# Second block: row splits shared by ScalarE and VectorE at three places, products of the identity in idle stretches of TensorE, and a reordered last layer norm of the first block

## What is computed

```python
for l in range(DEPTH):                      # block 1
    x = layer_norm(ALPHA * x + hybrid_mixer(x), ...)
    x = layer_norm(ALPHA * x + hier_moe(x), ...)
# block 2: u = norm(x) * (1 + scale) + shift, with a scale and a shift for each column
x = norm(ALPHA * x + gain * gla(u));  x = norm(ALPHA * x + gain * relu(u @ w1)**2 @ w2)
x = norm(ALPHA * x + gain * ssd(u));  x = norm(ALPHA * x + gain * relu(u @ w1)**2 @ w2)
```

## Time and profile before

| | us |
|---|---|
| three runs: median (lowest to highest) | 2241.13 (2236.27 to 2246.55) |
| the profiled execution: time / span | 2240.53 / 2238.3 |
| mean granted clock of TensorE | 0.961 of 2.4 GHz |
| TensorE (PE) busy | 2014.4 (90% of the span) |
| weight loads (PEld) busy | 1447.9 (65%) |
| VectorE (DVE) / ScalarE (ACT) / GpSimd (POOL) busy | 1229.2 / 729.5 / 167.2 |

### The profile page before, as it was taken

The page is one execution under the profiler, slowest core; times in us unless marked ns, Lnnn a source line. Parts: engine busy times, 40 slices in busy tenths (PEclk is TensorE's granted clock), DMA queues, the critical chain, the costliest instruction groups (busy, mean ns, idle before and its releaser), DMA issues.

```text
span 2238.3 us, 30881 instructions
## 1 busy us (share of the span) xinstructions
PE 2014.4 (90%) x12070; PEld 1447.9 (65%) x12070; DVE 1229.2 (55%) x2175; ACT 729.5 (33%) x1316; POOL 167.2 (7%) x155
## 2 busy tenths in 40 slices
PE   7989889879998778969998999999989988998997
PEld 4776433327785323326886788888867776777896
DVE  3474411134473212147466686666667876877676
ACT  3452201014552101124324311121165437654332
POOL 2001100001002000015422100000100000000000
PEclk9999999989998999988999999999999998999999
DMA  7589699975597899952221332232222342324552
GB/s 237 179 287 337 262 409 405 371 300 177 197 364 260 333 393 402 364 193 76 76 76 76 107 119 102 87 113 76 84 76 90 109 151 94 132 108 165 198 188 95
DMA packets 151921, 440.23 MB, mean 197 GB/s; under 512 B 10369, under 2 KB 12849, under 8 KB 143457
## 3 DMA queue, kind: packets, MB, share of 16 engines
q1 hardware_dynamic: 142704, 412.72, 49.3%
q0 software_dynamic: 8352, 22.39, 3.5%
q10 hardware_dynamic: 720, 3.15, 0.3%
HBM read 534.52 MB, written 1.21 MB: 239 GB/s over the span
## 4 chain that ended last, share of the span: by engine, by line
PE 40%; DVE 7%; ACT 4%; DVEq 2%; issue 1%; DMA 1%; ACTq 0%; POOL 0%; SPq 0%; POOLq 0%
PE bank L2117 22%; PE bank L2208 12%; PE bank L2259 4%; PE bank L2486 2%; DVE ARENA L3253 1%; ACT ARENA L2775 1%; PE bank L2122 1%; ACT ARENA L2768 0%; DVEq L2869 0%; ACT UT L2546 0%; ACTq L2549 0%; DMA W<-in_ffn_w 0%; DVE XA L2870 0%; DVEq L3255 0%; ACT ARENA L2523 0%
## 5 line engine op out<-in xcount | busy, mean ns | idle before, releaser
L2559 ACT ACTIVATE WPH<-W 128x1024 fp32r<-128x1024 f32 x128 | 135.5, 1063 | 379.5 <-PE bank L2117 198.1
L2117 PE MATMUL bank<-UH,WPH 128*128 128x512 f32 (+1 forms) x512 | 174.0, 340 | 6.8 <-DVE UL L2877 2.9
L2117 PE MATMUL bank<-UL,WPH 128*128 128x512 f32 (+1 forms) x512 | 172.7, 337 | 0.0
L2117 PE MATMUL bank<-UH,WPL 128*128 128x512 f32 (+1 forms) x512 | 172.7, 337 | 0.0
L2915 DVE TENSOR_TENSOR WPL<-W,WPH 128x1024 fp32r<-128x1024 f32 x128 | 153.4, 1219 | 17.9 <-ACT WPH L2559 17.9
L2208 PE MATMUL bank<-WPH,MHH 128*128 128x512 f32 x384 | 149.8, 390 | 0.0
L2208 PE MATMUL bank<-WPL,MHH 128*128 128x512 f32 x384 | 149.5, 389 | 0.0
L2208 PE MATMUL bank<-WPH,MHL 128*128 128x512 f32 x384 | 149.4, 389 | 0.0
L1431 DVE TENSOR_TENSOR H<-SG,bank 128x256 f32<-128x256 f32 x24 | 10.1, 421 | 235.9 <-ACT SG L1012 235.9
L2117 PE MATMUL bank<-ARENA 128*128 128x64 f32 (+4 forms) x528 | 105.7, 358 | 24.0 <-DVEq L3293 7.6
L710 PE MATMUL bank<-WC,H 128*32 128x512 f32 x768 | 93.7, 631 | 28.7 <-DMA WC<-in_expert_w_down 25.5
(11 more groups left out here) (460 smaller groups left out, 4266.8 us busy)
## 6 DMA issues: line engine op xcount, KB each, us to landing
WC<-in_expert_w_down SPq DMA_DIRECT2D x32, 2048.0 KB
W<-in_ffn_w SPq DMA_DIRECT2D x64, 1024.0 KB, 6.6
W<-in_ada_w SPq DMA_DIRECT2D x32, 1024.0 KB, 7.2
WA<-in_expert_w_gate SPq DMA_DIRECT2D x16, 2048.0 KB
WA<-in_expert_w_up SPq DMA_DIRECT2D x16, 2048.0 KB
W<-in_expert_w_gate SPq DMA_DIRECT2D x16, 2048.0 KB
W<-in_expert_w_up SPq DMA_DIRECT2D x16, 2048.0 KB
WC<-in_expert_w_down ACTq DMA_DIRECT2D x32, 1024.0 KB
```

The costliest lines, as they stand in the source:

```text
L2117: return nc.tensor.matmul(bank[r.bank(key)][0:rows, cols[0]:cols[1]], lhs, rhs, start=start, stop=stop)
L2559: nc.scalar.activation(piece_view(WPH, q), piece_src(i, q), ACT.Copy).then_inc(hi_done, 1)
```

## The change

In block 1: 18 products through the helper described above behind the last `combine` of the last layer, and the last layer norm done for both tiles together. In block 2: a helper that multiplies the identity with itself (128 columns, fp32) n times into a bank that it claims, called at eight places; and `SHARED`, four (tag, s) pairs at which for odd `j` ScalarE writes the high parts straight from the bank and VectorE computes `UT` from the bank before it subtracts.

```diff
@@ block1, TensorE
                 combine(l, MQ - 1)
+                if l == DEPTH - 1:
+                    keep_busy(("d", MQ - 1, 0), 18)
@@ block1, VectorE
+            def layer_norm_both(l, nth):
+                for t in range(TT):
+                    v.drain()
+                    nc.vector.bn_aggr(MV[:, t, :], BN[:, t, :, :].rearrange("p a b -> p (a b)"))
+                    v.drain()
+                    nc.vector.tensor_scalar(ST[:, 8 + t:9 + t], MV[:, t, 1:2], LN_EPS, None, ALU.add).then_inc(sq_in, 1)
+                v.wait_ge(ln_in, l * 64 + 32 * nth)
+                for t in range(TT):
+                    nc.vector.scalar_tensor_tensor(X[:, t, :], X[:, t, :], MV[:, t, 0:1], LN[:, 0, :], ALU.subtract, ALU.mult)
+                v.wait_ge(sq_out, 5 * l + 2 * nth + TT)
+                nc.vector.reciprocal(ST[:, 12:12 + TT], ST[:, 10:10 + TT])
+                v.drain()
+                for t in range(TT):
+                    nc.vector.scalar_tensor_tensor(X[:, t, :], X[:, t, :], ST[:, 12 + t:13 + t], LN[:, 1, :],
+                                                   ALU.mult, ALU.add).then_inc(x_ready, 1)
...
                     for n in range(2):
                         add_out(l, ("y", t, n), t, n)
-                    layer_norm(l, 2, t)
+                    if l < DEPTH - 1:
+                        layer_norm(l, 2, t)
+                if l == DEPTH - 1:
+                    layer_norm_both(l, 2)
@@ module
+SHARED = {("m0", 0), ("m0", 1), ("m1", 1), ("f1", 0)}
+def shared_turn(tag, s, j):
+    return (tag, s) in SHARED and j % 2 == 1
@@ block2, TensorE
+            def keep_busy(key, n):
+                r.claim(pe, key)
+                for _ in range(n):
+                    nc.tensor.matmul(bank[r.bank(key)][:, 0:P], ident[:], ident[:], start=True, stop=True)
...
-            def turned_x(tag, nt, snaked, before):
+            def turned_x(tag, nt, snaked, before, busy=(0, 0)):
                 for s in range(nt // 2):
+                    if busy[s]:
+                        keep_busy(("uT", tag, s, 0), busy[s])
                     if before is not None:
                         pe.wait_ge(x_rdy, before + 2 * s + 2)
...
-                turned_x(f"f{i}", nt, False, before)
+                turned_x(f"f{i}", nt, False, before, (0, 22) if i == 0 else (28, 0))
...
             key = ("ga",)
+            keep_busy(key, 28)
             pe.wait_ge(g_lo, 1)
...
+            keep_busy(("gy", 0, 0), 24)
             await_turned("o0")
...
-            turned_x("m1", 4, True, X_LN[0])
+            turned_x("m1", 4, True, X_LN[0], (12, 0))
             n = number[("dt",)] % SLOTS
             key = ("dt",)
+            keep_busy(key, 12)
             pe.wait_ge(dt_lo, 1)
...
+            keep_busy(("cb", 0), 44)
             pe.wait_ge(xd_rdy, NX + 2 * SG_)
             r.read(pe, ("xt", NX + SG_ - 1))
             group_pre(0)
             pe.wait_ge(x_whole, 1)
             group_gate(0)
+            keep_busy(("yo", 0), 52)
             for g in range(SG_):
@@ block2, ScalarE, split
                     r.filled(act, key)
+                    if shared_turn(tag, s, j):
+                        for k in (2 * j, 2 * j + 1):
+                            last = nc.scalar.activation(high[:, k, sl], bank[r.bank(key)][:, (k % 2) * SEQ:(k % 2 + 1) * SEQ],
+                                                        ACT.Identity, bias=acols[:, lay, kind, k, s:s + 1],
+                                                        scale=acols[:, lay, kind + 1, k, s:s + 1])
+                        last.then_inc(high_done, 1)
+                        continue
@@ block2, VectorE, lows
-            def lows(s, high, low, done, first):
+            def lows(tag, s, lay, kind, high, low, done, first):
...
                     v.wait_ge(high_done, first + 4 * s + j + 1)
+                    if shared_turn(tag, s, j):
+                        key = ("uT", tag, s, j)
+                        for k in (2 * j, 2 * j + 1):
+                            last = nc.vector.tensor_scalar(UT[:, k, sl], bank[r.bank(key)][:, (k % 2) * SEQ:(k % 2 + 1) * SEQ],
+                                                           acols[:, lay, kind + 1, k, s:s + 1], acols[:, lay, kind, k, s:s + 1],
+                                                           ALU.mult, ALU.add)
+                        r.read_done(last, key)
+                        v.drain()
```

More of the change, by code:

```diff
@@ L2970, in _ @@
             for s in range(2):
-                lows(s, XHG, XLO, g_xlow, 0)
+                lows("m0", s, 0, 0, XHG, XLO, g_xlow, 0)
             v.wait_ge(w2_in, 48)
@@ L3175, in gy_between @@
                     for s in range(2):
-                        lows(s, UH, UL, ul_done, 8)
+                        lows("f0", s, 0, 2, UH, UL, ul_done, 8)
             residual("gy", (), 4, 0, SQ_LN[0], None, gy_between)
             ffn(0, 4)
-            lows(0, XHI, XLO, x_low, 16)
+            lows("m1", 0, 1, 0, XHI, XLO, x_low, 16)
             n = number[("dt",)] % SLOTS
@@ L3185, in _ @@
                                     ALU.subtract).then_inc(dt_lo, 1)
-            lows(1, XHI, XLO, x_low, 16)
+            lows("m1", 1, 1, 0, XHI, XLO, x_low, 16)
             for b in range(2):
@@ L3377, in sy_between @@
                         low_part(1, q)
-                    lows(0, UH, UL, ul_done, 24)
+                    lows("f1", 0, 1, 2, UH, UL, ul_done, 24)
             residual("sy", (), 2, 0, SQ_LN[2], lambda t: ST[:, 36 + t:37 + t], sy_between)
```

## The result

The changed kernel measured 2251.66 us (median of 6 runs, 2246.69 to 2256.07) beside 2240.76 for the kernel before: a ratio of 1.004, 95% interval 1.0024 to 1.0055, so 5 to 12 us slower. A second round gave 1.0062 (1.0045 to 1.008). Forecast was 2241.6 us, with a range of 2233 to 2249. The profiled execution took 2251.93 us, its span is 2250.1.

A forecast was written before the change was run, and what follows sets the result against it. TensorE products of block 2 were taken to bound the kernel, partly at half clock. 6.1 - 2.7 - 1.7 - 0.8 - 0.6 + 0 + 0 + 0.8 = +1.1 us on 2240.5 gave 2241.6 us, range 2233 to 2249.

The forecast's parts named there:

- Block 1's end: Behind block 1's last combine: 18 products at 0.86 us each outlast the gap, so block 2 starts 6.1 us later.
- the first rival: At block 1's end: the call of 18 is hidden and block 2 starts at 992.0, total 2235.3 us; chance 0.13.
- LayerNorm: Block 1's last layer norm, done for both tiles together: 0 us, as TensorE arrives later anyhow.
- "m0" and "ga": Start of block 2, 28 products and shared splits: earlier start and 24 records at the high clock, 2.7 us gained.
- "gy": Block 2, idle from 1210.37, 24 products: filling ends 1.2 us late, records behind it run faster, 1.7 us gained.
- "f0": First feed-forward layer of block 2, 22 products: 0.15 us late, then low parts bind, 0.8 us gained.
- "m1" and "dt": Block 2, 12 products each, second pair shared: calls about as long as their gaps, 0.6 us gained.
- "cb" and "yo": Block 2, around the gate, 44 and 52 products: fillings end late, but cover and faster records cancel it, 0 each.
- the second rival: Group 0 in block 2: the clock falls again behind the filling at "yo", total 2246.3 us; chance 0.08.
- "f1": Second feed-forward layer of block 2, 28 products, shared: ScalarE starts 1.5 us late, 0.8 us lost in all.
- "gl": Early block 2, products behind "ga": still expected to show a half-clock stretch, with no gain counted.
- the third rival: At "gl": it stays at the high clock, 16 records taking 7.0 instead of 11.0 us, total 2237.6; chance 0.05.

The follow-up runs named there:

- run 16: Changed kernel with every turn split by ScalarE alone, nothing shared; 2248.81 us, ratio 1.0018 to the kernel before.
- run 4: Changed kernel without the call of 18 products at block 1's end; 2242.67 us, ratio 1.0001 to the kernel before.
- run 13: Changed kernel with the call at block 1's end cut from 18 products to 10; 2247.82 us, ratio 1.0013 to the kernel before.
- 10: Kernel before plus only the call of 18 at block 1's end and the joined LayerNorm, measured again; 2251.84 us, ratio 1.0046.
- 7: Kernel before plus only a call of 36 products at block 1's end, LayerNorm as it was; 2265.81 us, ratio 1.0102.
- 14: Changed kernel with a call of 26 products at block 1's end in place of 18; 2258.99 us, ratio 1.0065 to the kernel before.

## Why the prediction was wrong

The forecast was +1.1 us; the two rounds measured 10.4 and 12.0, and 2251.66 us lies 2.7 above the range. The loss of 6.1 us at block 1's end was forecast rightly. **The step that failed is the 5.0 us that the sum gives back for block 2** (2.7 + 1.7 + 0.8 + 0.6 - 0.8). In the runs the seven calls are worth 0.6 ± 0.7 and sharing costs 1.9 ± 0.7, so block 2 as a whole gives back nothing that these runs can measure. The terms, one by one, with the numbers of the changed kernel's profiles:

**Block 1's end: right.** 0.86 us a product and 6.1 us late; measured 0.87 and 6.4. It is the bulk of the loss, and the first rival (the call is hidden) is out. The page TensorE: Matmul & The Clock Gate of the Trainium skill, "Back-to-back issue gap", would have given 216 ns for each of these, as an estimate 3.9 us for the call, and the call for nothing. The 36 records in 15.71 us say 0.87 us a product: unsplit fp32 runs as two records here, each over twice as long as that. **LayerNorm: right,** 0 forecast, 0.4 ± 0.8 in the fit.

**"m0" and "ga", 2.7 us: what failed is "that fits beside ScalarE's pace of 2.6".** The profiles gain 1.1 of it, and with sharing taken out 0.5 more. "ga" waited for VectorE's low parts (0.45 us ahead of the last one), which the forecast had as not binding. I had priced VectorE's part from its lone 0.69 us and not from its first operations, which stand beside GpSimd's in the trace of before as well (three of them 4.32 us, as in run 16).

**"gy", 1.7 us: mis-sized by the call's own length.** Behind the call the records ran at the full clock as forecast (57.6 to 54.9 for the stage, 2.7 us). But the call was priced at the high clock, 5.4 us for 48 records, and the clock fell as it began, in both profiles (at 1217 and 1215). Timeline of the first, then of run 4, where the clock held:

```profile
1217.42 6.99 PE L2153 MATMUL bank<-ident 128*128 128x128 f32 x48
1224.16 0.48 PE L2298 MATMUL bank<-WHL,XHO 128*128 128x512 f32 x1
```

```profile
1206.06 5.52 PE L2151 MATMUL bank<-ident 128*128 128x128 f32 x48
1211.34 0.47 PE L2296 MATMUL bank<-WHL,XHO 128*128 128x512 f32 x1
```

From the last transpose ahead to "gy" it took 2.5 us more than before where 1.2 was forecast (0.9 in run 4), so that of the 1.7 only 0.2 is left. "gy" began at 1224.16, 9.6 us later than before, where the forecast has 6.1 - 2.7 + 1.2 = 4.6; the rest of that is the two stretches at 1182 and 1206, which are no part of the term.

**"f0": 0.8 forecast, 0.7 measured,** but three of the seven profiles of the unchanged block 2 took 350.6 us there without a call, against 350.5 with it and 351.3 in the forecast's own profile, so part of it may be chance. **"m1" and "dt", forecast 0.6 gained, lost 1.45:** the price of 0.112 a record. The clock fell behind the 6-column transposes, in both profiles, and 24 records took 4.27 us instead of 2.7:

```profile
1632.13 4.27 PE L2153 MATMUL bank<-ident 128*128 128x128 f32 x24 [0.42 <-ACT ARENA L2566]
```

In run 13, with the same two calls and the clock up in them (2.94 us), the stage gained 0.57 us, the forecast's own amount.

**"cb" and "yo", 0: right as a sum.** The call ran 4.6 us past the wait and the 40 records behind it took 6.32 instead of 10.64; the second rival (the clock falls again behind the call) didn't occur there. It did occur in other places, which it didn't name. **"f1", 0.8 lost: 1.3.** **"gl", the third rival:** half true; its half-clock stretch shrank from 13.7 to 10.2 us, and 1.7 us were gained that the forecast left at nothing.

**What the sum left out.** Where the clock falls behind a wait of 2 to 3 us that the change leaves open differs from one execution to the next. The four stretches at 1182, 1206, 1677 and 1712 cost the first profile about 6.6 us, by the stages in the table; the second profile has two of them, and kernels without the change have them as well. All gains were counted against one execution that had none of the four: its block 2 was the shortest of seven, 4.5 us under their mean. As a whole that execution was no rarity (38 of 139 runs of the kernel before were shorter, their mean is 2243). Block 1's end varies too, by 11 us (start of the last `combine` products, 971.4 to 982.1 in runs 10 and 7, from the same instructions).

The stretches that the change was made to fill were there in all seven profiles. So the luck of one profile explains some of the miss, and the terms above explain some. Means of profiles put it at this: block 2 took 1237.3 ± 1.1 us over the seven unchanged and 1235.0 ± 1.5 over the five with all of the change in it (the two of the changed kernel, 4, 13, 14). That would be 2.3 ± 1.9 us gained against 5.0 forecast, where the fit of the runs has 1.3 lost. Between a small gain and a small loss these runs can't decide. About 2 us of the changed kernel's surplus over the fit's 9.0 are unexplained too, and no clearer of its error.

## What to carry to other kernels

A filling product must be priced by a row of its own shape and precision, and at the half clock as well, since the clock can be down in the call itself. Its call must end before the wait does: 36 products at block 1's end stuck out by 22.0 us and cost 22.5, while what such calls bought in block 2 was too little to measure. Before a gain of some microseconds is worked out from half-clock stretches, profile the same kernel several times, see which stretches are always there and how long they are, and compare the stage with the mean of those profiles. Before work is moved from one engine to a second, look at what a third does beside it at that time.

## What the runs showed of the hardware

- The spread of a kernel's runs goes with that of its granted clock: the kernel before ran from 2234.4 to 2253.6 us in the 133 runs beside the experiments, and its mean clock from 0.965 down to 0.955, the longer runs at the lower clock (correlation -0.84).
- A wait of 2.4 us with the same length and the same work on both sides was followed by half clock in one execution and full clock in another.
- VectorE's 128x512 subtraction took 0.69 us with GpSimd idle, 3.13 us beside GpSimd's two of 128x256, which took 3.07, and 1.81 us beside one of 128x1024; it ended 0.56 and 0.55 us after GpSimd's.
- Products of the identity in fp32, 128 columns, 0.112 us a record at the full clock and about twice that at half, mostly held the clock; in both profiles of the changed kernel it fell at the start of the same two calls, at "gy" (1217 in the first) after a wait of 2.25 us and at "m1" (1633) behind the 6-column transposes, and in run 13 only at the first of them.
